# The last feed-forward group's down projection as block products, in a one-core float32 decoder layer

## What is computed

```
h_res = h_res + y
h = rms_norm(h_res, norm_mlp_g[i])
h_res = h_res + jnp.square(jax.nn.relu(h @ w_up[i])) @ w_down[i]     # 2048 x 8192, then 8192 x 2048
out = rms_norm(h_res, final_norm_g)
return out[:, N_META:]
```

## Time and profile before

| | before |
|---|---|
| median of 3 runs | 2284.91 (2282.47 to 2286.58) |
| the profiled execution's own time | 2283.76 |
| its span, first to last instruction | 2282.0 |
| TensorE busy, share of the span | 99% |
| mean granted TensorE clock | 0.999 |

### The profile page before, as it was taken

The page is one execution under the profiler, slowest core; times in us unless marked ns, Lnnn a source line. Parts: engine busy times, 40 slices in busy tenths (PEclk is TensorE's granted clock), DMA queues, the critical chain, the costliest instruction groups (busy, mean ns, idle before and its releaser), DMA issues.

```text
span 2282.0 us, 50606 instructions
## 1 busy us (share of the span) xinstructions
PE 2260.2 (99%) x19888; PEld 2109.2 (92%) x19888; DVE 1694.0 (74%) x2678; ACT 1110.6 (49%) x2076; POOL 299.7 (13%) x342
## 2 busy tenths in 40 slices
PE   8999999999999999999999999999999999999998
PEld 8999999999999788899999999999999999999888
DVE  7568577577586765588788778788788788787656
ACT  6534444344344423355555545555555455555436
POOL 5102012011020232200100001001001001001007
PEclk9999999999999999999999999999999999999999
DMA  8343343342442562535635636537447447357434
GB/s 253 82 107 83 95 97 85 94 109 70 110 96 81 148 188 81 173 104 136 159 102 138 140 102 157 140 91 166 123 111 167 120 113 170 97 132 196 140 102 153
DMA packets 513306, 286.07 MB, mean 125 GB/s; under 512 B 84526, under 2 KB 490544, under 8 KB 512688
## 3 DMA queue, kind: packets, MB, share of 16 engines
q1 hardware_dynamic: 478512, 224.19, 36.1%
q0 software_dynamic: 24080, 56.20, 11.2%
q10 hardware_dynamic: 10496, 2.62, 0.6%
HBM read 232.47 MB, written 50.47 MB: 124 GB/s over the span
## 4 chain that ended last, share of the span: by engine, by line
PE 91%; DVE 4%; DMA 2%; POOL 1%; ACT 1%; issue 1%; ACTq 0%; SPq 0%; POOLq 0%; DVEq 0%
PE PD L2152 17%; PE PD L2147 11%; PE PD L2402 10%; PE PD L2403 10%; PE PD L2404 10%; PE PW L2402 8%; PE PW L2403 8%; PE PW L2404 8%; PE PD L2368 1%; PE PD L2176 1%; PE PW L2176 1%; POOL acc L985 1%; PE PW L2226 1%; POOL psq L983 1%; DVE w_lo L1550 1%
## 5 line engine op out<-in xcount | busy, mean ns | idle before, releaser
L2152 PE MATMUL PD<-act_both,w_hi 128*128 128x264 f32 (+1 forms) x2496 | 412.7, 287 | 0.0
L2152 PEld LDWEIGHTS PD<-act_both,w_hi 128*128 128x128 f32 x2496 | 341.7, 188 | 11.5 <-issue 6.7
L2403 PE MATMUL PW<-uf,w_hi 128*128 128x256 f32 x1120 | 312.4, 279 | 0.0
L2402 PE MATMUL PW<-uf,w_hi 128*128 128x256 f32 x1120 | 312.4, 279 | 0.0
L2404 PE MATMUL PW<-uf,w_lo 128*128 128x256 f32 x1120 | 312.4, 279 | 0.0
L1036 ACT CAST w_hi<-w_sum 128x512 fp32r<-128x512 f32 x352 | 217.1, 617 | 181.2 <-PE PD L2404 121.2
L1503 DVE TENSOR_TENSOR w_lo<-w_sum,w_hi 128x512 fp32r<-128x512 f32 x352 | 240.4, 688 | 66.9 <-ACT w_hi L1036 65.1
L1550 DVE TENSOR_TENSOR w_lo<-w_raw,w_hi 128x512 fp32r<-128x512 f32 x268 | 200.5, 774 | 97.3 <-ACT w_hi L1052 93.8
L1052 ACT CAST w_hi<-w_raw 128x512 fp32r<-128x512 f32 x268 | 159.1, 619 | 209.4 <-DMA w_raw<-in_w_in 103.1
L2152 PE MATMUL PD<-act_both,w_lo 128*128 128x264 f32 (+1 forms) x1248 | 250.8, 282 | 0.0
L2403 PEld LDWEIGHTS PW<-uf,w_hi 128*128 128x128 f32 x1120 | 210.7, 188 | 0.3
(11 more groups left out here) (416 smaller groups left out, 5468.9 us busy)
## 6 DMA issues: line engine op xcount, KB each, us to landing
w_raw<-in_w_in SPq DMA_DIRECT2D x200, 256.0 KB, 3.1
w_raw<-in_w_down SPq DMA_DIRECT2D x136, 256.0 KB, 3.0
w_more<-in_w_down SPq DMA_DIRECT2D x136, 256.0 KB, 3.0
w_raw<-in_w_up SPq DMA_DIRECT2D x128, 256.0 KB, 3.1
w_more<-in_w_up SPq DMA_DIRECT2D x128, 256.0 KB, 3.3
residual<-form POOLq DMA_DIRECT2D x56, 512.0 KB, 7.5
w_raw<-in_w_out SPq DMA_DIRECT2D x64, 256.0 KB, 3.0
residual<-res POOLq DMA_DIRECT2D x2, 2048.0 KB, 10.1
```

Of the source, the lines that this page charges most:

```text
L2152: ins = M(PD[:, 2 * (n % 2) + a, cols], w, v[:, k, start:start + cols.stop - cols.start], start=begin, stop=end)
L2402: M(bank, whi, hi, start=begin, stop=False, skip_group_check=True)
L2403: M(bank, whi, lo, start=False, stop=False, skip_group_check=True)
```

## The change

`last_group` goes. The last group runs `mlp_group` and `down` like the others, for 6 pairs of output tiles (12 of 16 tiles, `BY_SEVEN`). The remaining four tiles (6, 14, 7, 15) are computed plainly, at the end, over tokens 0 to 255 and then 256 to 511: 8 steps of two slots, 24 matmuls over 256 tokens each.

- **Residual**: GpSimd reads it back in eight DMAs of one pair (512 KB) each, once the last up slot is used. VectorE adds each pair to it with one instruction over 128x1024 values behind the combination of p7 (`res_added`).
- **Squares**: behind each `res_added` GpSimd squares the pair (128x1024) and adds it to `acc2` (128x1024); for the first pair there is the squaring alone. The four plain tiles are squared by VectorE.
- **Rows**: 12 tiles are scaled, turned (four transposes each) and kept whole, 8 of them during pairs 2 to 5 of `down`, behind p6 and p4. The others are turned behind the plain steps.
- **One block of the activations** that the forms overwrite is stored to device memory during the up projection (128 KB per pair), read back, and split by two casts and two subtractions (`low_b12`) in the first plain step.

The core of the diff:

```
--- before.py
+++ after.py
+BY_SEVEN = 6
+END_TILES = [p + HALF_KT * x for p in range(BY_SEVEN, HALF_KT) for x in range(2)]
+END_STEPS = 2 * len(END_TILES)
+AHEAD_OF_END = 8
+TURNED_BEHIND = ((8,), (9,), (10, 11), (12,), (13,), (14, 15), (16, 17), (18,))
+SUM_BEHIND = 5
...
 GpSimd
-        pool.dma_start(res_a[:], res_view[:, 0:7, :]).then_inc(res_back, 16)
-        pool.dma_start(res_b[:], res_view[:, 7:14, :]).then_inc(res_back, 16)
-        pool.dma_start(res_c, res_view[:, 14:16, :]).then_inc(res_back, 16)
...
+        for u in range(HALF_UT):
+            pool.wait_ge(u_sq, UT * (FFG - 1) + 2 * u + 1)
+            pool.dma_start(b12_view[:, u, :], form[:, NP, :]).then_inc(b12_stored, 16)
+        pool.wait_ge(quarter_used, Q_DOWN)
+        for p in range(HALF_KT):
+            pool.dma_start(res_pair(p), res_view[:, p::HALF_KT, :]).then_inc(res_back[p // 4], 16)
+        pool.wait_ge(b12_stored, 16 * HALF_UT)
+        pool.dma_start(b12_back[:], b12_view).then_inc(b12_loaded, 16)
+        def pair_squares(p):
+            pool.wait_ge(res_added, p + 1)
+            if p == 0:
+                nc.gpsimd.tensor_tensor(acc2[:], res_pair(p), res_pair(p), ALU.mult).then_inc(acc_step, 1)
+                steps[0] += 1
+                return
+            pool.wait_ge(acc_step, steps[0])
+            nc.gpsimd.tensor_tensor(psq2[:], res_pair(p), res_pair(p), ALU.mult).then_inc(acc_step, 1)
+            pool.wait_ge(acc_step, steps[0] + 1)
+            nc.gpsimd.tensor_tensor(acc2[:], acc2[:], psq2[:], ALU.add).then_inc(acc_step, 1)
...
 ScalarE, in mlp_group
+                    if last and p >= 2 and i in (0, 2):
+                        gain_rows(2 * (p - 2) + i // 2)
+                    if last and p >= 2 and i in (4, 6):
+                        keep_rows(2 * (p - 2) + i // 2 - 2)
...
 VectorE, in mlp_group, behind p7's combination
+                        if last:
+                            dve.wait_ge(res_back[p // 4], 64)
+                            dve.wait_ge(combined, at(COMBINED_0 + N_COMBINED * (p + 1), N_COMBINED * HALF_KT, g))
+                            V.tensor_tensor(res_pair(p), res_pair(p), delta[:, p % 2].rearrange("p (a h) n -> p a (h n)", a=2),
+                                            ALU.add).then_inc(res_added, 1)
...
 VectorE, the plain tiles
+            for e in range(END_STEPS):
+                h, j = divmod(e, len(END_TILES))
+                m, n, cols = END_TILES[j], T_PLAIN + e, slice(h * NEAR, (h + 1) * NEAR)
+                end_split(2 * e + RM)
+                if e == 0:
+                    low_b12()
...
+                r = last_res(m)[:, cols]
+                dve.wait_ge(quarter_used, Q_PLAIN + 2 * (e + 1))
+                V.tensor_tensor(r, pd_seq(n)[:, 0:NEAR], r, ALU.add).then_inc(evacuated[n % 2], 1)
...
+                end_split(2 * e + RM + 1)
...
 TensorE
+                    if last and p >= 2 and product in ("p6", "p4"):
+                        turn_out(2 * (p - 2) + (product == "p4"))
...
+        down(FFG - 1, BY_SEVEN, last=True)
+        pe.wait_ge(fin_kept, AHEAD_OF_END)
+        for e in range(END_STEPS):
+            h, n = e // len(END_TILES), T_PLAIN + e
+            if e >= 2:
+                pe.wait_ge(evacuated[n % 2], free(n) - 1)
+            if e == len(END_TILES):
+                pe.wait_ge(b12_ready, 2)
+            for a in range(2):
+                i = I_PLAIN + 2 * e + a
+                pe.wait_ge(lo_split, R_LAST + i + 1)
+                for k in range(KQ):
+                    ins = multiply(pd_seq(n)[:, 0:NEAR], i, k, u_end(h, KQ * a + k, 0), u_end(h, KQ * a + k, 1),
+                                   begin=a == k == 0, end=a == 1 and k == KQ - 1)
+                ins.then_inc(quarter_used, 1)
+            for u in TURNED_BEHIND[e]:
+                turn_out(u)
+            if e == SUM_BEHIND:
+                pe.wait_ge(acc_step, ACC_STEPS + N_ACC)
+                pe.wait_ge(end_squared, 5)
+                pe.wait_ge(last_squared, 2)
+                sum_tokens(0, acc2[:, 0, 0:NEAR], acc2[:, 1, 0:NEAR], end_sq[:, 0, 0:NEAR], end_sq[:, 2, 0:NEAR])
```

More of the change, by code:

```diff
@@ L1336, in keep_next, with mlp_group @@
             keep_up(u + 1, i, g) if u < HALF_UT - 1 else keep_down(0, i, g)
-        def mlp_group(g):
+        def mlp_group(g, pairs=HALF_KT, last=False):
             def square(u, x):
@@ L1379, in mlp_group @@
                         keep_next(u, 1, g)
-            for p in range(HALF_KT):
+            for p in range(pairs):
                 for i in range(NP):
@@ L1386, in mlp_group @@
                     keep_down(p, i, g)
[L1387 to L1426, removed]
@@ new lines, in keep_rows, with round_b12 @@
+        def keep_rows(u):
+            m, t, n = UNITS[u]
+            act.wait_ge(fin_turned, u + 1)
+            nc.scalar.copy(rows[:, t:t + n, m * P:(m + 1) * P],
+                           unit_bank(u)[:, 0:n * P].rearrange("p (t n) -> p t n", n=P)).then_inc(fin_kept, 1)
+        def round_b12():
+            act.wait_ge(b12_loaded, 16)
+            act.wait_ge(quarter_used, Q_PLAIN)
+            for i in range(2):
+                nc.scalar.copy(b12_form(i, 0), b12_back[:, 2 * i:2 * i + 2, :]).then_inc(b12_hi_ready, 1)
@@ L1447, in _ @@
             mlp_group(g)
-        last_group()
+        mlp_group(FFG - 1, BY_SEVEN, last=True)
+        end_tiles()
         root_tokens(1)
@@ L2449, in up_pair, with down @@
                 ins.then_inc(quarter_used, 1)
-        def down(g):
+        def down(g, pairs=HALF_KT, last=False):
             whole = [(product, 0, KQ) for product in PRODUCTS]
@@ L2478, in down, with turn_out, sum_tokens @@
                         ins.then_inc(quarter_used, done)
+                    if last and p >= 2 and product in ("p6", "p4"):
+                        turn_out(2 * (p - 2) + (product == "p4"))
+        def turn_out(u):
+            m, first, n = UNITS[u]
+            pe.wait_ge(gained, u + 1)
+            if u < AHEAD_OF_END:
+                if u >= 2:
+                    pe.wait_ge(fin_kept, u - 1)
+            elif u >= AHEAD_OF_END + 4:
+                pe.wait_ge(fin_kept, u - 3)
+            else:
+                pe.wait_ge(combined, COMBINED_0 + N_COMBINED * (HALF_KT * (FFG - 1) + BY_SEVEN))
+            for t in range(n):
+                ins = nc.tensor.transpose(unit_bank(u)[:, t * P:(t + 1) * P], nt1[:, u % 3, t * P:(t + 1) * P], ident[:])
+            ins.then_inc(fin_turned, 1)
+        def sum_tokens(h, *parts, begin=True, end=True):
+            for t in range(2):
+                for i, squares in enumerate(parts):
+                    ins = M(PD[:, 1 + 2 * h, t:t + 1], squares[:, t * P:(t + 1) * P], ones2[:, 0:1],
+                            start=begin and t == i == 0, stop=end and i == len(parts) - 1, skip_group_check=True)
+            if end:
+                ins.then_inc(summed, 1)
         up_pair(0, 0, first=True)
@@ L2487, in _ @@
             up_pair(u, FFG - 1)
-        def turn_out(i):
-            pe.wait_ge(gained, i + 1)
-            if i >= 4:
-                pe.wait_ge(fin_kept, i - 3)
-            for t in range(2):
-                ins = nc.tensor.transpose(PW[:, i % 4, t * P:(t + 1) * P],
-                                          nt1[:, i % 3, t * P:(t + 1) * P], ident[:])
-            ins.then_inc(fin_turned, 1)
-        def sum_tokens(h, *parts, begin=True, end=True):
-            for t in range(2):
-                for i, squares in enumerate(parts):
-                    ins = M(PD[:, 1 + 2 * h, t:t + 1], squares[:, t * P:(t + 1) * P], ones2[:, 0:1],
-                            start=begin and t == i == 0, stop=end and i == len(parts) - 1, skip_group_check=True)
-            if end:
-                ins.then_inc(summed, 1)
@@ L2529, in _ @@
+        pe.wait_ge(end_squared, 10)
+        sum_tokens(1, acc2[:, 0, NEAR:SEQ], acc2[:, 1, NEAR:SEQ], end_sq[:, 0, NEAR:SEQ], end=False)
+        turn_out(len(UNITS) - 1)
         pe.wait_ge(last_squared, 3)
-        sum_tokens(1, sq_last2[:, NEAR:SEQ], begin=False)
+        sum_tokens(1, end_sq[:, 2, NEAR:SEQ], begin=False)
     ctx.close()
```

282 lines of the change are left out of this document (146 added, 136 removed).

## The result

The new kernel takes 2291.11 (median of 8 runs, 2289.36 to 2291.97) against 2284.21 for the kernel before (8 runs). The ratio is 1.0028, with a 95% interval of 1.0018 to 1.0039: slower by 4.1 to 8.9. The forecast was 2292, slower. The profiled execution took 2289.36, span 2287.6, so in the two profiled executions the difference is 5.6; the new kernel's is the fastest of its eight.

What follows compares the result with a forecast made beforehand. The prediction took TensorE, busy 99% of the span, as the bound, with VectorE slowed by GpSimd bounding the new pairs. Terms -8.8 + 10.1 + 5.0 + 1.0 = +7.3 gave 2291.1 for the profiled execution, median 2292, range 2278 to 2300.

Steps and rivals of the forecast that it cites:

- Up projection, -1.9: Last group's up projection: ScalarE's copy of p1 no longer queues behind the activations' cast, saving TensorE 1.9.
- TensorE's list, -8.8 in all: Last group to the end: up projection -1.9, down projection -6.6 and tail -0.3 together shorten TensorE's time by 8.8.
- VectorE's loss per pair, 3.8: Down projection pairs: GpSimd's squaring (1.7) and addition (2.1) hold VectorE back 3.8 a pair; bounds 0 and 4.9.
- Stalls in the pairs, +10.1: Last group's six pairs: VectorE needs 13.3 a pair against TensorE's 10.7, so they take 72.6 instead of 62.5.
- Gap ahead of plain step 2, +5.0: Plain steps: TensorE waits 5.0 before step 2 until VectorE has taken step 0 out of its bank.
- Clock, +1.0: Plain steps: the gap of 5.0 may lower TensorE's clock, costing between 0 and 16.8; 1.0 taken.
- Wait on `rows`, 1.4: Ahead of the plain steps TensorE waits 1.4 for unit 7 to be kept, behind ScalarE's cast and PSUM copy.
- its second term: Last group's down projection and plain steps: TensorE's work falls from 97.2 to 90.6, so -6.6.
- The residual's read-back at nothing: Down projection: the residual's DMAs land before pair 0's addition needs them, so they were costed at nothing.
- The rival in which the ports don't matter: Down projection: GpSimd falls into gaps, TensorE's list decides, no stall but the 1.4; -8.8, 2276, chance 0.16.
- the half absorbed one: Down projection: loss 2 to 2.5 a pair, stalls some 5 in pairs and 3 in plain steps; 2284, chance 0.22.

Runs made afterwards that it cites:

- the run above: Kernel before, with ScalarE's copies of the next pair's p1 and p5 in the last group placed as in other groups: 2281.64, ratio 0.9991 to the kernel before.
- no_squares: New kernel with GpSimd neither squaring nor adding the twelve tiles: 2276.77, ratio 0.9970 to the kernel before.
- memsets: New kernel with four GpSimd memsets over 128x1024 per pair in place of squaring and addition: span 2274.8, against the new kernel's 2287.6.
- square_only: New kernel with GpSimd squaring every pair but not adding the squares up: span 2277.4, against the new kernel's 2287.6.
- b12_later: New kernel with VectorE's split of the stored block in plain step 2 instead of step 0: span 2286.1, against the new kernel's 2287.6.
- gpsimd_adds: New kernel with ScalarE squaring each pair and GpSimd only adding the squares up: span 2284.3, against the new kernel's 2287.6.
- pieces: New kernel with GpSimd's squaring and addition of pairs 1 to 5 cut into four 128x256 pieces each: span 2281.2, against the new kernel's 2287.6.

## Why the prediction was right, step by step

- **Up projection, -1.9**: right, by the rows of the new kernel (2110.44 to 2172.56 is 62.12) and by the run above. In this group the gain has nothing to do with block products; it is the place of the copies of p1 and p5 in ScalarE's queue. The prediction named p1's alone.
- **TensorE's list, -8.8 in all**: too large by 1.3. no_squares has that list with its wait on `rows`: its median is 6.9 under before, and by its profile it is the 1.9 and 5.6 of stretch, -7.5. Its six pairs are as costed (62.4 for 62.5). Its plain steps take 27.7 to the last product matmul, for 26.7 costed. 0.6 of that is one price: the sums behind step 5 are 16 instructions in 1.68, since there are four parts for two token blocks and each fp32 matmul shows as two; I had read eight in 1.05. The rest lies spread over the steps and wasn't followed up.
- **VectorE's loss per pair, 3.8**: measured 3.9, with a round of 13.47 for 13.3. The extrapolation from 256 and 512 columns to 1024 held. That reading GpSimd instructions are the cause is shown by no_squares and memsets, the squaring's share by square_only (1.7, as costed).
- **Stalls in the pairs, +10.1**: from the first matmul of the six pairs to the last are 73.5 against 62.4 in no_squares, +11.1. In part this is near by luck. The forecast gave the last round the length of the others, 13.3, and let VectorE end 4.3 late, which TensorE doesn't feel; the last round was 10.70 and VectorE ended 1.3 late, and the two nearly cancel in this sum.
- **Gap ahead of plain step 2, +5.0**: the step that was mis-sized most, measured 1.9. The same last round is the reason. Behind pair 5 come plain slots, with no block sums to make, so VectorE's last round is 10.70 (2236.72 to 2247.42) and it comes out of the pairs 1.3 late, not 4.3, and that 3.0 is what the gap lacks. The mechanism was the one described, as b12_later shows.
- **Clock, +1.0**: nothing, as the gap was 1.9 and the granted clock stayed 1.00 behind it. In gpsimd_adds the gap was 2.8 and cost 1.3. The new kernel by window:

```profile
2254.00:2256.00 2.00, 0.19 (x2) 0.00 (x0) 2.00 (x3) 1.33 (x3) 0.58 (x1) 1.00 0.32 90
2256.00:2260.00 4.00, 3.88 (x33) 3.88 (x34) 3.90 (x9) 1.97 (x4) 0.00 (x0) 1.00 0.41 122
```

- **Wait on `rows`, 1.4**: 1.2 in the list, 1.4 in TensorE's cadence. The prediction costs it in its second term and yet says at its end that it has such a wait at nothing; the term is the one that came true. The residual's read-back at nothing: right, the addition of pair 0 follows its combination (2185.00, 2185.79) with no wait.

In the profiled executions the sum is -7.5 + 11.1 + 1.8 = +5.4 for the forecast's +7.3 (the gap counted by TensorE's cadence against no_squares; 5.6 between the two spans). The mechanism and VectorE's loss were right, and the median, 6.9 over the kernel before for some 7.1 forecast, is nearer than the terms are: a gain on TensorE that was 1.3 too large and stalls 1.0 too small stand against a gap and a clock term that were 4.2 too large together. That nearness is luck. Why the medians lie 1.5 further apart than the profiled terms isn't shown; the interval of 4.1 to 8.9 holds both.

The rival in which the ports don't matter is refuted by memsets against the new kernel; the half absorbed one by the rounds of 13.47.

## What to carry to other kernels

A change that shortens the busiest engine's list can be worth most of its price in matmuls and still lose, if it puts work in the path of the engine that feeds it: compare round times engine by engine (9.6 for VectorE alone, 10.7 for TensorE, 13.5 for VectorE with GpSimd beside it), not busy shares. Helper work on GpSimd that reads on-chip memory is not free beside VectorE instructions with two inputs in that memory; here the same squares on ScalarE and VectorE were worth 11.1 in the stretch. And work of the end (a split that is needed only four steps later, a copy one product too late in a queue) is worth a look once the big stall is gone: 2.5 here.

## What the runs showed of the hardware that I had not expected

- GpSimd's memsets, 3.99 for four over 128x1024, run beside VectorE's two-input instructions without slowing either: the low parts stay at 0.69. The same time spent on a squaring and an addition cost VectorE 3.9.
- A gap of 1.9 on TensorE left the granted clock at 1.00; one of 2.8 was followed by matmuls at the lower level (0.50 in the window, 1.2 GHz) for some 3 us, thirteen of them, at 0.213 instead of 0.117. Each is one execution; no run tried the gaps between.
- A VectorE instruction with one input in PSUM (L2044 in `pieces`, at 2216.45) took 0.41 beside one of GpSimd's reading pieces, as ever.
- Cutting GpSimd's instructions in four brought the loss from 3.9 to 3.1 and nearly doubled GpSimd's own time, 5.0 to 9.2.
